# The first microseconds of a decoder trunk: squares made by two engines, and a warm-up that needs no load

## What is computed

```python
def rmsnorm(x, g=None):
    xf = x.astype(jnp.float32)
    y = xf * lax.rsqrt(jnp.mean(xf * xf, axis=-1, keepdims=True) + EPS)
    if g is not None:
        y = y * g.astype(jnp.float32)
    return y.astype(x.dtype)
def modulate(h, shift, scale):
    return h * (1 + scale) + shift
def swiglu(h, wg, wu, wd):
    return (jax.nn.silu(h @ wg) * (h @ wu)) @ wd
# trunk, first lines of a layer
    silu_c = jax.nn.silu(c)
        mod = (silu_c @ p['w_ada'][l] + p['b_ada'][l]).reshape(B, N_MOD, D)
        hh = modulate(rmsnorm(x, p['g_pre'][l, 0]), m[0], m[1])
        f = swiglu(hh, p['w_ffn_gate'][l, 0], p['w_ffn_up'][l, 0], p['w_ffn_down'][l, 0])
```

## Time and profile before

| | us |
|---|---|
| Time, median of 3 runs (lowest to highest) | 1345.64 (1345.20 to 1345.84) |
| Time of the profiled execution | 1345.55 |
| Its span | 1343.9 |
| PE busy in it | 1315.2 (98%) |
| DVE, ACT, POOL busy | 786.9, 624.5, 115.4 |

### The profile page before, as it was taken

One profiled execution on the slowest core, in us unless ns is written; L12 is line 12 of the kernel. 1 busy time (PEld: TensorE's weight loads), 2 busy tenths in 40 slices (PEclk: granted clock), 3 DMA queues, 4 the chain that ended last, 5 costly groups with the idle time before them and its releaser, 6 DMA issues.

```text
span 1343.9 us, 24359 instructions
## 1 busy us (share of the span) xinstructions
PE 1315.2 (98%) x9746; PEld 1241.6 (92%) x9746; DVE 786.9 (59%) x1446; ACT 624.5 (46%) x1075; POOL 115.4 (9%) x207
## 2 busy tenths in 40 slices
PE   6999999999999999999999999999999999999998
PEld 4999999989975889999998999999988989999997
DVE  5544444578888875445456644445578895444443
ACT  5433334454544654343445543434468764443333
POOL 1100000023011130000001200000030120000000
PEclk9999999999999999999999999999999999999999
DMA  9765646447479736644544556454566834444342
GB/s 380 301 213 190 215 162 242 158 152 259 147 254 371 288 128 228 231 146 148 192 151 154 206 159 223 149 181 151 171 217 206 286 117 139 143 156 146 129 146 87
DMA packets 78641, 259.48 MB, mean 193 GB/s; under 512 B 10224, under 2 KB 20192, under 8 KB 77392
## 3 DMA queue, kind: packets, MB, share of 16 engines
q1 hardware_dynamic: 61664, 198.04, 43.5%
q0 software_dynamic: 16736, 59.44, 12.2%
q10 hardware_dynamic: 144, 0.66, 0.1%
HBM read 253.87 MB, written 4.23 MB: 192 GB/s over the span
## 4 chain that ended last, share of the span: by engine, by line
PE 87%; DVE 7%; DMA 2%; issue 2%; ACT 1%; POOL 0%; SPq 0%; DVEq 0%; ACTq 0%; POOLq 0%
PE ps L1729 27%; PE ps L1731 27%; PE ps L1730 27%; PE ps L1797 2%; DMA lent_lo<-in_ada 2%; DVE w_lo L2305 2%; DVE f L2390 1%; DVE f L2373 1%; PE ps L1354 1%; DVE x L2377 0%; DMA ones_d<-in_ones_d 0%; PE ps L1893 0%; DVE f L2395 0%; DVE xn_lo L2385 0%; PE ps L848 0%
## 5 line engine op out<-in xcount | busy, mean ns | idle before, releaser
L1729 PE MATMUL ps<-xn_hi,w_hi 128*128 128x320 f32 x1800 | 564.5, 314 | 9.7 <-DVE xn_lo L2385 7.6
L1731 PE MATMUL ps<-xn_hi,w_lo 128*128 128x320 f32 x1800 | 556.2, 309 | 0.0
L1730 PE MATMUL ps<-xn_lo,w_hi 128*128 128x320 f32 x1800 | 556.1, 309 | 0.0
L2305 DVE TENSOR_TENSOR w_lo<-w_raw,w_hi 128x1024 fp32r<-128x1024 f32 (+1 forms) x357 | 382.0, 1107 | 112.1 <-ACT w_hi L2077 111.7
L2077 ACT ACTIVATE w_hi<-w_raw 128x1024 fp32r<-128x1024 f32 x362 | 330.7, 959 | 76.4 <-PE ps L1731 72.9
L1729 PEld LDWEIGHTS ps<-xn_hi,w_hi 128*128 128x128 f32 x1800 | 337.9, 188 | 25.5 <-issue 11.4
L1730 PEld LDWEIGHTS ps<-xn_lo,w_hi 128*128 128x128 f32 x1800 | 338.1, 188 | 0.4
L1731 PEld LDWEIGHTS ps<-xn_hi,w_lo 128*128 128x128 f32 x1800 | 337.9, 188 | 0.0
L1729 PE MATMUL ps<-mid_hi,w_hi 128*128 128x320 f32 x704 | 218.2, 310 | 0.3 <-DVE w_lo L2305 0.3
L1730 PE MATMUL ps<-mid_lo,w_hi 128*128 128x320 f32 x704 | 217.4, 309 | 0.0
L1731 PE MATMUL ps<-mid_hi,w_lo 128*128 128x320 f32 x704 | 217.4, 309 | 0.0
(11 more groups left out here) (339 smaller groups left out, 1032.0 us busy)
## 6 DMA issues: line engine op xcount, KB each, us to landing
w_raw<-in_gu SPq DMA_DIRECT2D x176, 512.0 KB, 4.7
a_raw<-in_ada POOLq DMA_DIRECT2D x76, 512.0 KB, 7.0
w_raw<-in_down SPq DMA_DIRECT2D x64, 512.0 KB, 3.6
w_raw<-in_pj SPq DMA_DIRECT2D x57, 512.0 KB, 4.8
w_raw<-in_down SPq DMA_DIRECT2D x64, 192.0 KB, 3.6
ex_xn<-in_ada POOLq DMA_DIRECT2D x16, 512.0 KB, 6.0
w_raw<-in_ada SPq DMA_DIRECT2D x16, 512.0 KB, 6.6
front<-in_front SPq DMA_DIRECT2D x5, 1024.0 KB, 13.7
```

What stands on the lines that cost most here:

```text
L1729: pe.matmul(out, hi, xhi, start=start, stop=False)
L1730: pe.matmul(out, hi, xlo, start=False, stop=False)
L1731: return pe.matmul(out, w_lo[s][:, w_at:w_at + P], xhi, start=False, stop=stop)
L2305: dve.tensor_tensor(w_lo[s][:, cols], w_raw[:, s, cols], w_hi[s][:, cols].bitcast(F32), ALU.subtract).then_inc(w_split, 1)
```

## The change

PE's wait for `c_silu` moves from the start of its stream into `front_sums(0)`. The warm-up takes five products instead of three, on tile 0 of `f`, which DVE has cleared for it, and waits for that alone (`f_clear`). `ones_d` becomes the first of POOL's loads, with a semaphore of its own (`mean_in`); `ident` (`const_in`) is second and awaited ahead of `spread`. ACT makes the squares of tiles 0 to 4 only; DVE makes those of tiles 5 to 7, then adds 5 to 1, 6 to 2, 7 to 3 and 4 to 3. PE sums four tiles of `sqx` (0 to 3) instead of two, the first as soon as it is there.

```diff
+FILLS = 5
+SQUARED = 5
...
+        f_clear, mean_in = sem("f_clear"), sem("mean_in")
...
         def small_loads(gp):
 
+            gp.dma_start(ones_d[:, :], t["ones_d"]).then_inc(mean_in, 16)
             gp.dma_start(ident[:, :], t["ident"]).then_inc(const_in, 16)
-            gp.dma_start(ones_d[:, :], t["ones_d"]).then_inc(const_in, 16)
...
-            def fill(n):
+            def fill(n, src):
 
                 for _ in range(n):
-                    pe.matmul(ps[:, 3, 0:TOK], ident[:, :], x[:, 0, :], start=True, stop=True)
+                    pe.matmul(ps[:, 3, 0:TOK], src[:, 0, 0:P], src[:, 0, :], start=True, stop=True)
 
             def front_sums(c):
 
+                if c == 0:
+                    pe.wait_ge(c_silu, 1)
                 pe.wait_ge(piece_landed[c], 16)
...
-                pe.wait_ge(const_in, 16 * 2)
-                pe.wait_ge(x_in[0], 16)
-                fill(3)
+                pe.wait_ge(f_clear, 1)
+                fill(FILLS, f)
+                pe.wait_ge(mean_in, 16)
                 stat_x("gate0")
                 front_sums(0)
                 pe.wait_ge(sel_in, 16)
+                pe.wait_ge(const_in, 16)
                 spread(x_stat("gate0"), rx3, B_RY)
                 front_turn(0)
-                fill(2)
+                fill(2, x)
                 front_sums(1)
...
             def stat_x(prep):
 
-                for r in range(2):
-                    pe.wait_ge(sqx_added, r + 1)
-                    last = token_sums(B_YSUM, 0, sqx[:, r, :], r == 0, r == 1)
+                pe.wait_ge(sqx_ready, 1)
+                token_sums(B_YSUM, 0, sqx[:, 0, :], True, False)
+                for r in range(1, 4):
+                    pe.wait_ge(sqx_added, r)
+                    last = token_sums(B_YSUM, 0, sqx[:, r, :], False, r == 3)
                 last.then_inc(stat_done, 1)
...
             pe.sem_inc(w_used, CR)
-            pe.wait_ge(c_silu, 1)
             pe.sem_inc(sel_done, 2)
...
             def squares_x(prep):
-                for k in range(KC):
+                for k in range(SQUARED):
                     act.wait_ge(x_in[2 * k // KC], 16)
                     act.activation(sqx[:, k, :], x[:, k, :], ACT.Square).then_inc(sqx_ready, 1)
...
             def sum_squares():
 
-                added = {}
-                for k in range(2, KC):
-                    r = k % 2
-                    dve.wait_ge(sqx_ready, k + 1)
-                    if k >= 4:
-                        steps.wait(added[k - 2])
-                    both = dve.tensor_tensor(sqx[:, r, :], sqx[:, r, :], sqx[:, k, :], ALU.add)
-                    if k < KC - 2:
-                        added[k] = steps.did(both)
-                    else:
-                        both.then_inc(sqx_added, 1)
+                def add(r, k):
+                    return dve.tensor_tensor(sqx[:, r, :], sqx[:, r, :], sqx[:, k, :], ALU.add)
+
+                dve.wait_ge(x_in[1], 16)
+                for k in range(SQUARED, KC):
+                    own = steps.did(dve.tensor_tensor(sqx[:, k, :], x[:, k, :], x[:, k, :], ALU.mult))
+                steps.wait(own)
+                for r in (1, 2):
+                    dve.wait_ge(sqx_ready, r + 1)
+                    add(r, r + 4).then_inc(sqx_added, 1)
+                dve.wait_ge(sqx_ready, 4)
+                steps.did(add(3, 7))
+                steps.wait()
+                dve.wait_ge(sqx_ready, SQUARED)
+                add(3, 4).then_inc(sqx_added, 1)
...
             dve.memset(eps[:, :], EPS)
+            dve.memset(f[:, 0, :], 0.0).then_inc(f_clear, 1)
             dve.memset(c32[:, :, :], 0.0).then_inc(c_zero, 1)
```

## The result

The kernel before took 1345.69 us (median of 11 runs, 1345.2 to 1348.76), the changed one 1348.93 us (11 runs, ten of them between 1348.5 and 1349.8, one at 1346.98). Changed over before is 1.002, 95% interval 1.0013 to 1.0028: slower by about 3 us. The prediction was 1345.5 us with a range of 1344.2 to 1347.2, and the measured time lies above it. The profiled execution took 1348.56 us, with a span of 1346.9. Rival C of the prediction, a fall of the clock, stood at 1348.0 (1347 to 1349).

The account below looks back on a forecast made before the run. The prediction took PE, busy 98% of the span, as the bound, with transfers of pieces 3 and 4 limiting its start: 1345.55 - 0.1 = 1345.45, median 0.09 higher, so 1345.5 us, range 1344.2 to 1347.2.

Parts of the forecast that it names:

- Rival C: Around piece 3: PE idles 1.5 to 2.6 us, the clock falls; 1348.0 us (1347 to 1349), chance 0.15.
- The head: Warm-up and token sums: PE starts near 2.0, sums done 1.0 to 2.5 us earlier than 13.4.
- What is late next: Pieces 1 and 3: PE waits for their landings; an instruction fetch delays piece 3 from 22.7 to 23.8.
- The step behind it: From piece 3's sums to piece 4's: 3.09 us, so piece 4's start moves by -0.3 to +0.1 us.
- C's own price: Behind the wait for piece 3: half of some 4.8 us of work at 1.2 GHz is lost, +2.4 us.
- The transfers take the gain back: At pieces 3 and 4: their landings undo nearly all of the head's gain, leaving -0.1 us.
- B: At the front pieces: transfers don't bind, the whole 2.5 us head gain comes through; 1343.1 us, chance 0.08.
- A: Between pieces 3 and 4: no lagging engine, piece 4 lands near 25.2, a gain of 0.9; 1344.7 us, chance 0.15.
- D: Token sums: clock low again, head gains 1.0 not 2.5 us, same time as forecast; chance 0.62 together with the forecast.

Follow-up runs that it names:

- e4: The kernel before with nine tiny products (36 PE instructions) ahead of everything; median 1347.04 us, ratio 1.0007 to before.
- e17: The changed kernel with fillers (unneeded products) only: seven in the warm-up, three ahead of piece 1's sums, four ahead of piece 3's; 1345.97 us, ratio 0.9996.
- e2: The changed kernel with the old squares, additions and two-tile sums, so the warm-up part alone; 1347.78 us, ratio 1.0011.
- e13: e9 with seven instead of five fillers in the warm-up and one instead of two ahead of piece 1's sums; 1345.6 us, ratio 0.9992.
- e15: e13 without the three fillers ahead of tile(0, 2); 1348.24 us, ratio 1.0010.
- e6: The changed kernel with another order on TensorE, tile(0, 2) ahead of piece 3's sums, without added fillers; 1346.47 us, ratio 1.0006.
- e7: e6 with three fillers between tile(0, 1) and tile(0, 2); 1346.25 us, ratio 1.0003.
- e12: The changed kernel with two fillers between tile(0, 1) and piece 3's sums; 1345.93 us, ratio 0.9996.
- e9: e7 with ScalarE's Silu table load moved behind its copy of piece 5's sums; 1345.6 us, ratio 0.9995.
- e5: The changed kernel with piece 3 loaded ahead of the second half of weight tile 1; 1348.89 us, ratio 1.0017.
- e1: The changed kernel with four fillers between tile(0, 1) and piece 3's sums; 1346.99 us, ratio 1.0002.
- e8: e4 with two fillers between tile(0, 1) and piece 3's sums; 1346.0 us, ratio 1.0000 to before.
- e16: e9 with seven instead of five fillers in the warm-up and three instead of two ahead of piece 1's sums; 1343.93 us, ratio 0.9984.
- e14: The changed kernel with seven instead of five fillers in the warm-up; 1348.86 us, ratio 1.0018.

## Why the prediction was wrong, point by point

- *The head* was right. Warm-up from 1.98 to 7.68 (predicted 2.0 to 7.6), token sums done at 11.2 (10.9 to 12.4). PE went on 0.04 to 0.07 us behind a landing, where the prediction had 0.2; that changed nothing.
- *What is late next* was right. Piece 1's sums at 15.25 (15.4), `tile(0, 1)` over at 21.5 (21.4), the instruction packet at 21.5 to 22.0 (19 to 22.5), piece 3 there at 23.94 (23.8), its sums at 23.98 (23.9 to 24.0). e4, made to test it, delayed piece 3 by 1.7 us with 36 instructions alone (the changed kernel: 1.2). The wait of 2.48 us was in the predicted 1.5 to 2.6.
- *The step behind it* is what failed. The sum took 3.09 us for the step from piece 3 to piece 4, its length at 2.4 GHz, and with that put at nothing what the wait ahead of it costs through the clock. Piece 4's sums were to start at 26.6 to 27.05. They started at 28.31, 4.33 us later than piece 3's, because from 25.1 us on the work ran at 1.2 GHz; with work in the waits and nothing else changed (e17) the same step took 3.09. Every number up to there was the forecast's own, and they made the wait certain that rival C asks for. C still had only 0.15, and the prediction gives no reason for that: no row of the kernel before showed a wait of over 1.2 us behind the start, and the lack of such a row left the chance open.
- *C's own price* was a little small: 4.8 us of work at the low level and 2.4 us lost, from the first rise. Measured are 6.7 and 2.9, because the clock fell at 25.1 and came back only at 31.8. Such a stretch has no fixed length: it was 3.4 us in the traces of e2 and e4, 6.8 in that of e13 and over 13 in that of e15, where other waits lay inside it. With 0.15 for C and its price at 2.4 the range ended at 1347.2, below every run of the changed kernel but one.
- *The transfers take the gain back* was right, and shown by e17: with the clock kept, piece 4's sums start at 27.20, 0.3 later than before (forecast: 0.1 earlier, bounds -0.3 to +0.1), of which the fillers have 0.13, since they held piece 3's sums until 24.11. The median of the nine runs is 1345.85, 0.3 to 0.4 us above the runs of before that kept the clock. B, that the transfers don't bind, is refuted. So is A: piece 4 landed at 26.4 again, issued at 6.24 and 20.2 us on the way, where A had 25.2. With the packet ahead of piece 3's end, pieces 3 and 4 land 2.5 us apart instead of 3.7.
- *D*, the clock low in the token sums or behind them, happened in the profiled runs of e6, e7 and e12, where the sums of piece 0 took 1.94 us. It did not in the changed kernel's profile, so whether the wait for piece 3 would hide it there, as the prediction has it, isn't shown. In e7 it wasn't hidden: piece 3's sums started at 26.36, in e9, which kept the clock, at 24.43.
- The Trainium skill ("TensorE: Matmul & The Clock Gate", HAM oscillation — how this bites in real kernels) describes a loop that waits for an operand's transfer and starts its next tile at half rate. The trace of e13 agrees: behind 1.28 us of waiting the sums of piece 1 ran at the low level from their start (1.93 us). In the changed kernel and in e4, behind 2.48 and 0.94 us, the first group behind the wait still ran at the high level (1.07 us), and the fall came 1.1 and 2.3 us after work had resumed.

## What to carry to other kernels

When an edit makes PE earlier ahead of a transfer that doesn't move, the new wait is not free: ask what clock the work behind it will run at, and price the next 3 to 7 us of it at the low level. Fill such a wait with real work from further on, or with products into an unused bank, and do so at every wait of the stretch; with one left open (e13) four of 11 runs still lost 2.5 us or more against the best. All fillers here were products of 128x128 on 320 columns; whether smaller ones would do wasn't tried. And before an order is changed, follow the in-order queues of the other engines: two of these experiments (e5, e7) lost what they were to gain behind a weight split and a table load on ScalarE.

## What was not expected of the hardware

- A wait of 0.94 us in a stretch of small products was followed by the low clock in the trace of e4, and half of its runs have such a time; so were two waits in the attention stage in the profiles of e1 (0.64 us each, 1.3 us lost) and e17 (0.64 and 1.05). Wide products in such waits of the head went with a mean clock of 0.999 or more in 10 of 10 runs (e8) and 9 of 11 (e16, e17).
- The length of a wait doesn't decide alone. Behind some 1.3 us the clock fell at piece 1 (e13), with small products and one filler ahead of the wait, and held at the turn of piece 5 (e7), with passes of tiles ahead of it.
- The fall can come after work has resumed: in the changed kernel the sums of piece 3, from 23.98, ran at full speed and the turn at 25.56 did not. In e5 and e13 it came inside the wait.
- An instruction fetch of 0.02 MB, in a queue that moves 420 GB/s, made a 1 MB load 1.1 to 1.8 us later, depending only on whether it came ahead of its end.
- The mean granted clock of a run, to three digits, sorted most of the runs that the median mixes. A comparison of medians here says as much on how often the clock was kept as on the work.
- What stays open: which waits lose the clock and which don't (e12 against e4, e9 against e14), where the six slower runs of e2 lost it, and the group of runs of the kernel before that is 3 us longer at a mean clock of 0.999.
